# One kernel of a two-layer sequence model: compression, compressed attention and the choice of blocks written as one stage

## The chip, the cores and the metric

The kernel runs on one core of a Trainium2 chip. The metric is the device time of one launch in microseconds (us); lower is better.

## The reference

The whole model has two layers of attention and two feed-forward blocks on 1,024 tokens of width 1,024. The change touches one part of the second attention layer, whose 16 heads in 4 groups attend in three ways. The part in question is the compressed way and the choice of blocks:

```python
n_cmp = (S - CMP_LEN) // CMP_STRIDE + 1          # 63 windows of 32 tokens, one every 16
cidx = arange(n_cmp)[:, None] * CMP_STRIDE + arange(CMP_LEN)[None, :]
def compress(t, pe, w1, w2):                     # t: 4 groups x 1024 tokens x 64
    blocks = t[:, :, cidx] + pe
    blocks = blocks.reshape(Bn, C_KV_HEADS, n_cmp, CMP_LEN * HEAD_DIM)
    return silu(blocks @ w1) @ w2                # 2048 -> 128 -> 64
k_cmp = rms_norm(compress(kc, cmp_pe[0], cmp_w1[0], cmp_w2[0]), k_gain[0])
v_cmp = compress(vc, cmp_pe[1], cmp_w1[1], cmp_w2[1])
s_c = q @ k_cmp * scale - slopes * dist_c        # masked where dist_c < 0
p_c = softmax(s_c)                               # zero where a token sees no window
o_cmp = p_c @ v_cmp
importance = einsum('bgjtn,nm->bgtm', p_c, overlap)    # 16 blocks of 64 tokens
score = where(blk > cur, -inf, where(forced, inf, importance))
top_s, top_i = top_k(score, 8)                   # blocks for the selected attention
```

## The kernel before

The program is a row of stages. Each has its own buffers and semaphores, one instruction stream for each engine, and ends with a barrier of all engines, so that no stage overlaps the next. TensorE is "PE", VectorE "DVE", ScalarE "ACT", GpSimd "POOL", and SyncE "SP" issues most DMAs.

Between the projection stage `in1` and the attention stage `at1` of the second layer stand, in this order:

- three short mask stages (`distance_bias_stage`, and `bias_parts_stage` twice), which the change leaves as they are and only moves;
- `compress_stage` ("cmp"). SP loads `w1s` and `t_in` for keys and values. Both have the 64 channels of a head on 64 partitions. PE waits for all six loads, then multiplies each of the 32 steps of the window by the position embedding (`ps_b`, L1819, one moving column) and by the strided windows of the four groups (`ps_h`, L1825, 252 moving columns), for keys and for values. Each full fp32 matmul shows as two instructions in the trace. A short chain of Silu, the second matrix, the norm and a transposition gives `kcT` and `vc`;
- `select_stage` ("sel"). It handles one group (4 heads) and one tile of 128 tokens at a time: 32 rounds, with the tiles `n` and the groups in one order on every engine. `q` is loaded with 66 rows for each head (64 channels and two rows that carry the distance term). In each round PE makes `transposes(n)`, `values(n-1)`, `scores(n+2)`; DVE makes `normalize(n)`, from the fifth token tile on `pick(n)` (the sum over heads, the sum over windows, the eighth largest, the mark), `output(n-1)` and `negate(n+2)`; ACT makes four exponentials with their sums and one copy out of PSUM;
- `transposed_selection_stage` ("selT"), which transposes the marks of all tokens and stores them in DRAM for `at1` through the POOL queue.

The lines of the round are: L1954 scores, L1964 transposes, L1974 values, L2032 mask added, L2035 maximum, L2001 exponentials, L2046 probabilities, L2056 to L2072 the choice, L2081 the gated output.

Of the kernel before, what the change touches and what calls it, by code (L numbers as in the profile page):

```python
# [1751 lines left out]
def compress_stage(nc, kvT, pe, w1, w2, k_gain, gate_cols, kcT, vc, gates, ident):  # L1752


    G = KV_HEADS
    NW = N_CMP
    with Stage(nc, "cmp") as st:
        t_in = st.sb("t_in", [HD, 2, G, SEQ])
        w1s = st.sb("w1s", [HD, 2, CMP_LEN, CMP_HIDDEN])
# [10 lines left out]
        root = st.sb("root", [NW, G])  # L1770
        rstd = st.sb("rstd", [NW, G])
        pos_i = st.sb("pos_i", [CMP_PAD, 1], I32)
        ktok = st.sb("ktok", [CMP_PAD, G, HA])
        ps_h = st.ps("ps_h", [CMP_HIDDEN, 2, BANK])
        ps_b = st.ps("ps_b", [CMP_HIDDEN, 2, BANK])
        ps_c = st.ps("ps_c", [CMP_PAD, 2, BANK])
        ps_t = st.ps("ps_t", [P, 1, BANK])
        pe_in, in_sem, g_in, gain_in = st.sem("pe_in"), st.sem("in"), st.sem("g_in"), st.sem("gain_in")
        peT_ready, peT_done, bias_ready, pb_done, hid_ready, hid_done, c_ready = (
            st.sem(x) for x in ("peT_ready", "peT_done", "bias_ready", "pb_done", "hid_ready", "hid_done", "c_ready"))  # L1780
# [557 lines left out]
```

## Time and profile before

| | |
|---|---|
| median of three runs | 4008.2 us (4007.9 to 4011.0) |
| the profiled execution | 4013.1 us, of it 4011.1 us span |
| busy share of the span | PE 86%, weight loads (PEld) 72%, DVE 41%, ACT 30%, POOL 3% |
| `cmp`, first DMA to the next stage | 2173.1 to 2285.4 us |
| `sel` | 2285.4 to 2507.3 us |
| `selT`, up to the first instruction of `at1` | 2507.3 to 2519.2 us |
| mask stages ahead of `cmp` | 2161.7 to 2173.0 us |

Times are counted from the start of the span. The profile names each instruction by its line and its tiles, written out<-in. "PEclk" is the granted TensorE clock: 1.00 is 2.4 GHz and 0.50 is 1.2 GHz. Busy shares are averages over stages with different limits. Because a barrier closes each stage, the time of a stage is the time of its own longest chain.

### The profile page before, as it was taken

To read this page: it belongs to the slowest core of one execution; us is meant where nothing else is said; L and a number is where in the kernel's file an instruction comes from. 1 tells how busy PE (TensorE), PEld (TensorE's weight loads), DVE (VectorE), ACT (ScalarE), POOL (GpSimd) and SP (SyncE) were. 2 spreads that over 40 slices of the span, in tenths; PEclk is the share of its full clock that TensorE was granted. 3 is DMA by queue.
4 is the path that set the end of the run, shared out by engine and by line. 5 is a ranking of instruction groups with operands and counts; after the bars stand their busy time and mean duration, and the time that the engine had idled before them with its cause. 6 is when DMAs were issued, how large, how long until landed. Compare 5 with 4: busy or idle time off the path is not lost. (4 is left out here: it accounts for less than half of the span.)

```text
span 4011.1 us, 46382 instructions
## 1 busy us (share of the span) xinstructions
PE 3463.5 (86%) x17061; PEld 2898.9 (72%) x17061; DVE 1654.7 (41%) x3187; ACT 1222.4 (30%) x2492; POOL 118.3 (3%) x152
## 2 busy tenths in 40 slices
PE   5997673776889999997996877699999879999998
PEld 4886563665778888886886666588788668888887
DVE  3133784445223232324430044588788332323323
ACT  3233332333122121223331132466566222221211
POOL 0000000000000000000000000111111000000000
PEclk8998786888999999998995555899999989999999
DMA  3344001332022121212733000321120111212112
GB/s 116 100 106 113 16 6 40 68 64 67 6 63 74 58 70 57 74 45 62 175 91 66 22 22 0 65 62 32 33 63 1 42 48 53 74 53 79 63 59 84
DMA packets 262495, 239.79 MB, mean 60 GB/s; under 512 B 41928, under 2 KB 203720, under 8 KB 262280
## 3 DMA queue, kind: packets, MB, share of 16 engines
q1 hardware_dynamic: 262200, 236.67, 22.1%
q8 instruction: 135, 2.21, 0.2%
q0 software_dynamic: 80, 0.26, 0.1%
q14 instruction: 80, 0.66, 0.1%
HBM read 191.58 MB, written 45.29 MB: 59 GB/s over the span
## 5 line engine op out<-in xcount | busy, mean ns | idle before, releaser
L498 PE MATMUL ffn_acc<-ffn_hT_hi,ffn_w_hi 128*128 128x512 f32 x1408 | 435.9, 391 | 17.5 <-DVE ffn_w_lo L579 17.5
L498 PE MATMUL ffn_acc<-ffn_hT_lo,ffn_w_hi 128*128 128x512 f32 x1408 | 435.3, 390 | 0.0
L498 PE MATMUL ffn_acc<-ffn_hT_hi,ffn_w_lo 128*128 128x512 f32 x1408 | 434.8, 390 | 0.0
L579 DVE TENSOR_TENSOR ffn_w_lo<-ffn_raw,ffn_w_hi 128x1024 fp32r<-128x1024 f32 x88 | 107.9, 1226 | 738.5 <-ACT ffn_w_hi L538 738.5
L1153 PE MATMUL in_acc<-in_w_hi,hT_hi 128*128 128x512 f32 (+1 forms) x832 | 330.4, 397 | 14.8 <-DVE in_w_lo L1233 14.8
L1637 ACT ACTIVATE at_pr<-at_ps_s 128x512 f32<-128x512 f32 x480 | 224.2, 467 | 335.2 <-PE at_ps_s L1570 332.8
L1155 PE MATMUL in_acc<-in_w_hi,hT_lo 128*128 128x512 f32 (+1 forms) x832 | 325.6, 391 | 0.0
L1154 PE MATMUL in_acc<-in_w_lo,hT_hi 128*128 128x512 f32 (+1 forms) x832 | 324.9, 391 | 0.0
L538 ACT ACTIVATE ffn_w_hi<-ffn_raw 128x1024 fp32r<-128x1024 f32 x88 | 93.3, 1060 | 750.1 <-PE ffn_acc L498 737.2
L1696 DVE TENSOR_TENSOR at_p_lo<-at_pr,at_p_hi 128x512 fp32r<-128x512 f32 x480 | 273.0, 586 | 110.2 <-ACT at_p_hi L1644 109.7
L498 PEld LDWEIGHTS ffn_acc<-ffn_hT_hi,ffn_w_hi 128*128 128x128 f32 x1408 | 265.4, 189 | 73.1 <-DVE ffn_w_lo L579 18.1
L498 PEld LDWEIGHTS ffn_acc<-ffn_hT_lo,ffn_w_hi 128*128 128x128 f32 x1408 | 265.6, 189 | 55.5
L498 PEld LDWEIGHTS ffn_acc<-ffn_hT_hi,ffn_w_lo 128*128 128x128 f32 x1408 | 265.4, 189 | 55.3
L1686 DVE TENSOR_REDUCE at_top<-at_ps_m 128x1 f32<-128x512 f32 (+1 forms) x480 | 243.7, 526 | 129.6 <-PE at_ps_m L1550 126.5
L518 PE MATMUL ffn_acc_d<-ffn_d_hi,ffn_a_hi 128*128 128x512 f32 x704 | 273.9, 389 | 0.0
L519 PE MATMUL ffn_acc_d<-ffn_d_lo,ffn_a_hi 128*128 128x512 f32 x704 | 273.9, 389 | 0.0
L520 PE MATMUL ffn_acc_d<-ffn_d_hi,ffn_a_lo 128*128 128x512 f32 x704 | 273.9, 389 | 0.0
L1550 PE MATMUL at_ps_m<-at_kc,at_qa 128*128 128x512 f32 (+1 forms) x480 | 177.0, 382 | 112.0 <-DMA at_qb<-q0T_lo 37.3
L1644 ACT ACTIVATE at_p_hi<-at_pr 128x512 fp32r<-128x512 f32 x480 | 237.9, 497 | 0.0
L1550 PEld LDWEIGHTS at_ps_m<-at_kc,at_qa 128*128 128x128 f32 x480 | 95.1, 198 | 143.8 <-issue 83.4
L1153 PEld LDWEIGHTS in_acc<-in_w_hi,hT_hi 128*128 128x128 f32 x832 | 165.5, 199 | 45.6 <-DVE in_w_lo L1233 17.1
L549 ACT ACTIVATE ffn_d_hi<-ffn_d_raw 128x512 fp32r<-128x512 f32 x176 | 108.4, 629 | 277.9 <-PE ffn_acc_d L520 277.9
(307 smaller groups left out, 6090.8 us busy)
## 6 DMA issues: line engine op xcount, KB each, us to landing
ffn_d_raw<-in_ffn_w_down SPq DMA_DIRECT2D x176, 256.0 KB, 2.8
ffn_raw<-in_ffn_w_gate SPq DMA_DIRECT2D x44, 512.0 KB
ffn_raw<-in_ffn_w_up SPq DMA_DIRECT2D x44, 512.0 KB
in_raw<-in_hy_w_in SPq DMA_DIRECT2D x56, 256.0 KB
proj<-in_nat SPq DMA_DIRECT2D x40, 256.0 KB, 2.1
in_raw<-in_nsa_w_in SPq DMA_DIRECT2D x40, 256.0 KB
sel_q<-q1T SPq DMA_DIRECT2D x16, 264.0 KB
at_qa<-q1T_hi SPq DMA_DIRECT2D x16, 264.0 KB
```

The costliest lines, as they stand in the source:

```text
L498: ins = nc.tensor.matmul(acc[:, m, half, :], w[:, m, k, :], h[:, k, half * HALF:(half + 1) * HALF], start=k == 0 and w is w_hi and h is hT ...
L518: nc.tensor.matmul(acc_d[:, x, :], a_hi[:, k, rows], d_hi[:, n % R, :], start=k == 0, stop=False)
L519: nc.tensor.matmul(acc_d[:, x, :], a_hi[:, k, rows], d_lo[:, n % R, :], start=False, stop=False)
L520: ins = nc.tensor.matmul(acc_d[:, x, :], a_lo[:, k, rows], d_hi[:, n % R, :], start=False, stop=k == G - 1)
L1153: nc.tensor.matmul(acc[:, n % 4, 0:cols], x_hi, r_hi, start=k == 0, stop=False)
L1154: nc.tensor.matmul(acc[:, n % 4, 0:cols], x_hi, r_lo, start=False, stop=False)
L1155: ins = nc.tensor.matmul(acc[:, n % 4, 0:cols], x_lo, r_hi, start=False, stop=k == KD - 1)
L1550: ins = nc.tensor.matmul(ps_m[:, m % 2, pos * P:(pos + n) * P], lhsT, rhs, start=x == 0, stop=x == len(parts) - 1, skip_group_check=True)
L1637: nc.scalar.activation(pr[:, c % R, 0:w], ps_s[:, c % RB, 0:w], ACT.Exp).then_inc(p_done, 1)
L1644: nc.scalar.activation(p_hi[:, c % R, 0:w], pr[:, c % R, 0:w], ACT.Copy).then_inc(hi_done, 1)
L1686: ins = nc.vector.tensor_reduce(top[:, u, half, x:x + 1], ps_m[:, m % 2, 0:w * P], AX.X, ALU.max)
L1696: nc.vector.tensor_tensor(p_lo[:, c % R, 0:w], pr[:, c % R, 0:w], p_hi[:, c % R, 0:w].bitcast(F32), ALU.subtract).then_inc(lo_done, 1)
```

## The change

The three stages become one, `compress_select_stage` ("cmpsel"), which stands ahead of the mask stages.

- Compression works with 128 rows: steps 0 to 15 of the window on partitions 0 to 63 and steps 16 to 31 on partitions 64 to 127. For that `t_in` holds the tokens twice, the second time shifted by 16. There are 16 matmuls for keys and 16 for values, each with 258 moving columns: 256 windows and two columns for the position embedding. Keys have their own wait (`k_in`), and values theirs (`v_in`).
- `q` holds two heads on 128 partitions, without the rows of the distance term. `kcp` and `vcp` hold the compressed keys and values of a group twice, block-diagonally, so that one matmul of 128x128 serves two heads.
- A round is a tile of 128 tokens with all 16 heads: 8 rounds instead of 32. Each has 8 head pairs in `scores`, `transposes` and `values`, and DVE works on 128x1024 elements at a time.
- The distance term is made by POOL (`make_bias`) and added by DVE. POOL subtracts the maximum, ACT makes one exponential of 128x1024, and DVE sums it with a reduction.
- `ps_t` and `ps_o` are no longer doubled; `ps_s` is.
- The marks are transposed for the last four token tiles only, and stored through the SP queue inside the same stage.

```diff
...
+def compress_select_stage(nc, kvT, pe, w1, w2, k_gain, gate_cols, qT, gates, selT, mixed, ident, slopes):
...
+        t_in = st.sb("t_in", [P, 2, COLS + 2 * HALF])
+        w1s = st.sb("w1s", [P, 2, HALF, CMP_HIDDEN])
...
+        kcp = st.sb("kcp", [P, G, P])
+        vcp = st.sb("vcp", [P, G, P])
+        q = st.sb("q", [P, PAIRS, SEQ])
...
+        ps_s = st.ps("ps_s", [P, 2, 2 * BANK])
+        ps_t = st.ps("ps_t", [P, 2, BANK])
+        ps_o = st.ps("ps_o", [P, 2, BANK])
...
+            for v, done in ((0, k_in), (1, v_in)):
+                kv = kvT[v * G:(v + 1) * G, 0:HD, :].rearrange("g r t -> r g t")
+                to = t_in[:, v, 0:COLS].rearrange("p (g t) -> p g t", g=G)
+                wv = w1[v, :, :].rearrange("(e l d) h -> e d l h", e=2, d=HD)
+                for half in range(2):
+                    rows = slice(half * HD, half * HD + HD)
+                    sp.dma_start(w1s[rows, v, :, :], wv[half]).then_inc(done, 16)
+                    sp.dma_start(to[rows, :, 0:SEQ - half * HALF], kv[:, :, half * HALF:SEQ]).then_inc(done, 16)
...
+            for n in range(2):
+                tok = slice(n * BANK, (n + 1) * BANK)
+                for half in range(2):
+                    of = qT[:, 0:HD, tok].rearrange("(j e) r t -> e r j t", e=2)[half]
+                    sp.dma_start(q[half * HD:half * HD + HD, :, tok], of).then_inc(q_in[n], 16)
+            sp.wait_ge(selT_taken, 1)
+            sp.wait_ge(blocks_set, 1)
+            sp.dma_start(selT.rearrange("g b t -> (g b) t"), blocks[:].bitcast(F32)).then_inc(sel_out, 16)
+            sp.wait_ge(sel_out, 16)
...
+            def make_bias(i):
...
+                nc.gpsimd.tensor_tensor(bias[:, i % 2, :, :],
+                                        dist[:, i % 2, :].rearrange("p (o n) -> p o n", o=1).to_broadcast([P, C_HEADS, CMP_PAD]),
+                                        bcast(nslope[:].rearrange("p (h o) -> p h o", o=1), CMP_PAD), ALU.mult).then_inc(bias_step, 1)
+                pool.wait_ge(bias_step, i + 1)
+                nc.gpsimd.affine_select(out=bias[:, i % 2, :, :], in_=bias[:, i % 2, :, :], compare_op=ALU.is_ge, fill=NEG,
+                                        base=i * P - (CMP_LEN - 1), pattern=[[0, C_HEADS], [-CMP_STRIDE, CMP_PAD]],
+                                        channel_multiplier=1).then_inc(bias_done, 1)
...
+            make_bias(0)
+            make_bias(1)
+            for i in range(TT):
+                pool.wait_ge(top1_done, i + 1)
+                nc.gpsimd.tensor_tensor(s[:, i % 2, :, :], s[:, i % 2, :, :],
+                                        bcast(top1[:, i % 2, :].rearrange("p (h o) -> p h o", o=1), CMP_PAD), ALU.subtract)\
+                    .then_inc(sub_done, 1)
+                if i + 2 < TT:
+                    make_bias(i + 2)
...
+            for v, done in ((0, k_in), (1, v_in)):
+                te.wait_ge(done, 64)
+                for l in range(HALF):
+                    windows = t_in[:, v, l:l + CMP_STRIDE * (NW + 1) + 1:CMP_STRIDE]
+                    ins = nc.tensor.matmul(ps_s[:, 0, v * BANK:v * BANK + NW + 2], w1s[:, v, l, :], windows, start=l == 0,
+                                           stop=l == HALF - 1)
...
+            def scores(i):
+                if i % 4 == 0:
+                    te.wait_ge(q_in[i // 4], 32)
+                if i >= 2:
+                    te.wait_ge(biased, i - 1)
+                for m in range(PAIRS):
+                    ins = nc.tensor.matmul(ps_s[:, i % 2, m * P:(m + 1) * P], q[:, m, i * P:(i + 1) * P], kcp[:, m // 2, :],
+                                           start=True, stop=True)
+                ins.then_inc(s_done, 1)
+
+            def transposes(i):
+                te.wait_ge(pn_done, i + 1)
+                if i:
...
+                for m in range(PAIRS):
+                    ins = nc.tensor.transpose(ps_t[:, m // 4, (m % 4) * P:(m % 4 + 1) * P], rows[:, m, :], ident[:])
+                ins.then_inc(t_done, 1)
...
+            def values(i):
+                te.wait_ge(pt_done, i + 1)
...
+                for m in range(PAIRS):
+                    ins = nc.tensor.matmul(ps_o[:, m // 4, (m % 4) * P:(m % 4 + 1) * P], pt[:, i % 2, m, :], vcp[:, m // 2, :],
+                                           start=True, stop=True)
+                ins.then_inc(o_done, 1)
+
+            scores(0)
+            scores(1)
+            for i in range(TT):
+                transposes(i)
+                if i:
+                    values(i - 1)
+                if i + 2 < TT:
+                    scores(i + 2)
+            values(TT - 1)
+            te.wait_ge(biased, TT)
+            te.wait_ge(sel_done, TT - FIRST)
+            for i in range(FIRST, TT):
+                ins = nc.tensor.transpose(ps_s[0:G * N_SLC, 0, (i - FIRST) * P:(i - FIRST + 1) * P],
+                                          sel[:, i - FIRST, :, :].rearrange("p g n -> p (g n)"), ident[:])
+            ins.then_inc(selT_ready, 1)
...
+                    nc.scalar.activation(hid_v[:, :, 0, :], of.rearrange("p (g n) -> p g n", g=G), ACT.Silu, bias=pb[:, 1:2])
+                    nc.scalar.activation(hid_v[:, :, 1, :], of.rearrange("p (g n) -> p g n", g=G), ACT.Silu, bias=pb[:, 1:2])\
...
+            nc.scalar.activation(gates[:], g_raw[:], ACT.Sigmoid).then_inc(norm, 1)
+            act.wait_ge(c_ready, 2)
+            act.wait_ge(zeroed, 2)
+            for half in range(2):
+                rows = slice(half * HD, half * HD + HD)
+                nc.scalar.activation(vcp[rows, :, rows], ps_o[rows, 1, 0:G * HD].rearrange("p (g d) -> p g d", d=HD), ACT.Copy)\
+                    .then_inc(vcp_done, 1)
+
+            def exps(i):
+                act.wait_ge(sub_done, i + 1)
+                nc.scalar.activation(s[:, i % 2, :, :], s[:, i % 2, :, :], ACT.Exp).then_inc(e_done, 1)
...
+                nc.scalar.activation(pt[:, i % 2, :, :], ps_t[:].rearrange("p b (m c) -> p (b m) c", c=P), ACT.Copy).then_inc(pt_done, 1)
...
+            act.wait_ge(selT_ready, 1)
+            act.wait_ge(blocks_set, 1)
+            nc.scalar.activation(blocks[:, FIRST * P:SEQ], ps_s[0:G * N_SLC, 0, 0:SEQ - FIRST * P], ACT.Copy).then_inc(selT_taken, 1)
...
+            dve.wait_ge(norm, 4)
+            nc.vector.reciprocal(rstd[:], root[:]).then_inc(norm, 1)
+            dve.wait_ge(norm, 5)
+            for half in range(2):
+                ins = nc.vector.tensor_tensor(ktok[:, :, half, :], ps_o[0:CMP_PAD, 0, 0:G * HD].rearrange("p (g d) -> p g d", d=HD),
+                                              bcast(rstd[:].rearrange("p (g o) -> p g o", o=1), HD), ALU.mult)
...
+            for half in range(2):
+                rows = slice(half * HD, half * HD + HD)
+                nc.vector.tensor_scalar(kcp[rows, :, rows], ps_t[rows, 0, 0:NW].rearrange("p (g n) -> p g n", n=CMP_PAD),
+                                        gain[rows, 0:1], None, ALU.mult).then_inc(kcp_done, 1)
...
+            def maxima(i):
+                dve.wait_ge(s_done, i + 1)
+                dve.wait_ge(bias_done, i + 1)
...
+                nc.vector.tensor_tensor(s[:, i % 2, :, :], ps_s[:, i % 2, :].rearrange("p (h n) -> p h n", n=CMP_PAD),
+                                        bias[:, i % 2, :, :], ALU.add).then_inc(biased, 1)
...
+                nc.vector.tensor_reduce(top1[:, i % 2, :], s[:, i % 2, :, :], AX.X, ALU.max).then_inc(top1_done, 1)
...
+            def normalize(i):
...
+                nc.vector.tensor_reduce(rowsum[:, i % 2, :], s[:, i % 2, :, :], AX.X, ALU.add).then_inc(link, 1)
+                dve.wait_ge(link, at + 1)
+                nc.vector.reciprocal(rl[:, i % 2, :], rowsum[:, i % 2, :]).then_inc(link, 1)
...
+                nc.vector.tensor_tensor(pn[:, i % 2, :, :], s[:, i % 2, :, :],
+                                        bcast(rla[:, i % 2, :].rearrange("p (h o) -> p h o", o=1), CMP_PAD), ALU.mult)\
+                    .then_inc(pn_done, 1)
...
+            def pick(i):
...
+                nc.vector.tensor_reduce(both[:, :, 1:], pn[:, i % 2, :, :].rearrange("p (g j) n -> p g n j", g=G), AX.X, ALU.add)\
...
+            def output(i):
+                dve.wait_ge(o_done, i + 1)
...
+                nc.vector.tensor_tensor(mixed[:, i, :].rearrange("p (h d) -> p h d", d=HD),
...
+            maxima(0)
+            maxima(1)
+            for i in range(TT):
+                normalize(i)
+                if i >= FIRST:
+                    pick(i)
+                if i:
+                    output(i - 1)
+                if i + 2 < TT:
+                    maxima(i + 2)
+            output(TT - 1)
...
+                compress_select_stage(nc, kvT, nsa_cmp_pe[0, :, :, :], nsa_cmp_w1[0, :, :, :], nsa_cmp_w2[0, :, :, :],
+                                      nsa_k_gain[0, 0, :], proj1[:, main:ODD_IN], q1T, gates, selT, mixed, ident,
+                                      slopes(C_HEADS, 0, C_HEADS))
                 masks = []
...
-                compress_stage(nc, kvT, nsa_cmp_pe[0, :, :, :], nsa_cmp_w1[0, :, :, :], nsa_cmp_w2[0, :, :, :],
-                               nsa_k_gain[0, 0, :], proj1[:, main:ODD_IN], kcT, vc, gates, ident)
-                select_stage(nc, q1T, kcT, vc, gates, sel, mixed, ident)
...
-                transposed_selection_stage(nc, sel, selT, ident)
...
```

The seven operations of `pick(i)` are those of before on 128x4x64 and 128x4x16 elements; `max` and `match_replace` run four times, once for each group.

## Rows read from the trace of the kernel before

**Rows 1.** The page's slices: the granted clock in 40 equal slices.

```profile
PEclk8998786888999999998995555899999989999999
```

**Rows 2.** Windows by stage: length, busy us (instructions), clock, DMA share, GB/s.

```profile
core 0: us, PE busy (x) PEld busy (x) DVE busy (x) ACT busy (x) POOL busy (x), PEclk, DMA share, GB/s
2173.00:2197.80 24.80, 0.31 (x1) 0.13 (x1) 0.22 (x1) 0.00 (x0) 1.36 (x12) 0.50 1.00 181
2197.80:2225.10 27.30, 27.27 (x128) 27.27 (x129) 0.00 (x0) 0.00 (x0) 0.00 (x0) 0.50 0.00 1
2225.10:2279.90 54.80, 54.80 (x130) 39.07 (x131) 0.00 (x0) 1.95 (x4) 0.00 (x0) 0.50 0.00 0
2279.90:2285.40 5.50, 2.47 (x20) 2.04 (x20) 1.97 (x6) 4.12 (x6) 0.00 (x0) 0.50 0.00 0
2293.40:2507.30 213.90, 153.14 (x640) 130.74 (x640) 92.70 (x320) 66.09 (x289) 0.00 (x0) 0.50 0.05 14
```

**Rows 3.** Timeline of one of 32 rounds: start, us, engine, line, operation, idle before.

```profile
2489.53 0.43 DVE L2046 TENSOR_TENSOR sel_pn<-sel_e,sel_rla 128x256 f32<-128x256 f32 x1
2489.99 0.60 DVE L2056 TENSOR_REDUCE sel_both<-sel_pn 128x64 f32<-128x256 f32 x1
2490.11 1.03 PE L1964 MATMUL sel_ps_t<-ident,sel_pn 128*64 128x128 f32 x4 [1.88 <-DVE sel_pn L2046]
2491.07 1.97 PE L1974 MATMUL sel_ps_o<-vc,sel_pt 64*128 x8
2492.05 0.17 DVE L2072 TENSOR_SCALAR sel<-sel_marked 128x16 f32 x1 [0.15 <-DVE sel_marked L2070]
2492.97 1.97 PE L1954 MATMUL sel_ps_s<-kcT,sel_q 66*128 x8
2494.97 0.42 DVE L2032 TENSOR_TENSOR sel_s<-sel_ps_s,sel_cmask 128x256 f32<-128x256 f32 x1 [1.33 <-PE sel_ps_s L1954]
2496.24 0.43 DVE L2046 TENSOR_TENSOR sel_pn<-sel_e,sel_rla 128x256 f32<-128x256 f32 x1
```

**Rows 4.** Windows: the transfer rate of the first loads, nothing else running.

```profile
2176.00:2196.00 20.00, 0.00 (x0) 0.00 (x0) 0.21 (x1) 0.00 (x0) 0.00 (x0) 0.50 1.12 205
```

**Rows 5.** Timeline: the end of `cmp`, table load and sigmoid.

```profile
2282.84 1.28 ACT L1853 ACT_TABLE_LOAD   x1
2284.13 0.52 ACT L1853 ACTIVATE gates<-cmp_g_raw 128x384 f32<-128x384 f32 x1
```

**Rows 6.** Groups by form, whole kernel: busy us, mean ns, idle before.

```profile
L920 DVE TENSOR_TENSOR hg_q<-hg_ps_tr,hg_q 128x1024 f32<-128x1024 f32 x4 | 4.9, 1225 | 5.5 <-ACT hg_q L845 5.5
L1240 DVE TENSOR_REDUCE in_ss<-in_sq 128x8 f32<-128x512 f32 x32 | 22.0, 687 | 86.2 <-ACT in_sq L1195 86.2
L1529 POOL TENSOR_TENSOR at_shift<-ident,at_top 128x512 fp32r<-128x512 f32 x80 | 91.5, 1143 | 747.1 <-DVE at_top L1690 747.1
L1520 POOL TENSOR_SCALAR_AFFINE_SELECT at_base<-at_base 128x1024 f32<-128x1024 f32 x2 | 2.1, 1038 | 0.1
L838 ACT ACTIVATE hg_kl<-hg_kl 128x1024 f32<-128x1024 f32 x4 | 4.2, 1056 | 0.1
```

**Rows 7.** Windows in other stages, for the clock.

```profile
424.40:428.20 3.80, 3.80 (x18) 3.80 (x19) 0.00 (x0) 0.00 (x0) 0.00 (x0) 0.50 0.02 4
428.20:442.00 13.80, 13.71 (x124) 13.52 (x123) 6.60 (x12) 5.15 (x7) 0.00 (x0) 1.00 0.01 2
473.20:482.30 9.10, 0.00 (x0) 0.00 (x0) 8.98 (x15) 0.03 (x1) 0.00 (x0) 0.66 0.64 173
1857.00:1865.20 8.20, 6.80 (x30) 6.00 (x31) 7.39 (x11) 3.58 (x6) 0.00 (x0) 0.50 0.01 2
1865.20:1868.90 3.70, 1.71 (x13) 1.24 (x12) 3.70 (x5) 2.27 (x4) 0.00 (x0) 0.96 0.00 0
```

**Rows 8.** Timeline: the marks' store and the next stage.

```profile
2513.92 0.69 POOL L2188 DMA_DIRECT2D selT<-selT_blocks  x1 [226.39 <-ACTq L67]
2519.15 0.94 POOL L1515 MEMSET at_base<- 128x1024 f32 x1 [4.54 <-POOLq L70]
```

More of the change, by code:

```diff
@@ L1747, in _ @@
             rounds(dve, body)
[L1752 to L1759, printed above, removed]
+def compress_select_stage(nc, kvT, pe, w1, w2, k_gain, gate_cols, qT, gates, selT, mixed, ident, slopes):
+    G, J = KV_HEADS, GROUP
+    HALF = CMP_LEN // 2
+    COLS = G * SEQ
+    NW = G * CMP_PAD
+    PAIRS = C_HEADS // 2
+    FIRST = TOPN * SLC // P
+    PICKED = 3e38
+    FORCED = 1e30
+    with Stage(nc, "cmpsel") as st:
+        t_in = st.sb("t_in", [P, 2, COLS + 2 * HALF])
+        w1s = st.sb("w1s", [P, 2, HALF, CMP_HIDDEN])
@@ L1770, in compress_stage @@
[L1770 to L1780, printed above, removed]
@@ L1812, in _ @@
             te.wait_ge(pe_in, 16)
-            nc.tensor.transpose(ps_t[0:HD, 0, 0:2 * CMP_LEN], pes[:], ident[0:2 * CMP_LEN, 0:2 * CMP_LEN]).then_inc(peT_ready, 1)
-            te.wait_ge(in_sem, 16 * 6)
-            te.wait_ge(peT_done, 1)
-            for v in range(2):
-                for l in range(CMP_LEN):
-                    ins = nc.tensor.matmul(ps_b[:, v, 0:1], w1s[:, v, l, :], peT[:, v * CMP_LEN + l:v * CMP_LEN + l + 1],
-                                           start=l == 0, stop=l == CMP_LEN - 1)
-                ins.then_inc(bias_ready, 1)
@@ L1822, in _ @@
[L1822 to L1833 removed]
+            for v in range(2):
+                ins = nc.tensor.transpose(ps_t[:, 1, v * HALF:(v + 1) * HALF], pes[:, v, :, :].rearrange("l e d -> l (e d)"),
+                                          ident[0:HALF, 0:HALF])
@@ new lines, in _ @@
+            te.wait_ge(w2_in, 16)
+            te.wait_ge(hid_done, 1)
+            for g in range(G):
+                ins = nc.tensor.matmul(ps_o[0:CMP_PAD, 0, g * HD:(g + 1) * HD], hid_k[:, g, :], w2s[:, 0, :], start=True, stop=True)
+            ins.then_inc(c_ready, 1)
+            te.wait_ge(hid_done, 2)
+            for g in range(G):
+                ins = nc.tensor.matmul(ps_o[:, 1, g * HD:(g + 1) * HD], hid_v[:, g, :, :].rearrange("p e n -> p (e n)"), w2s[:, 1, :],
+                                       start=True, stop=True)
```

421 lines of the change are left out of this document (147 added, 274 removed).

## The prediction
> **What bounds the kernel now.** I read the page's slices first, then windows cut at the stage borders, then the timeline of one round. The slices put four tenths of a millisecond at half clock [rows 1]: it is this part of the program. The windows then say what each stage waits for [rows 2]. First 24.8 us of transfers with PE idle; then 27.3 and 54.8 us in which PE is busy throughout at clock 0.50; a chain of 5.5 us; and 213.9 us of rounds in which PE is busy for 153.1 us and no other engine for more than 92.7. With the load of `q` and `selT` it is 346.1 us, from 2173.0 to 2519.15 [rows 8]. A barrier closes every stage, so what is saved here is saved in the total.
>
> The round shows why PE at 72% still sets the pace [rows 3]. `pn` ends at 2489.96; PE transposes, multiplies values and makes scores until 2494.94; then DVE adds the mask, takes the maximum and normalizes, and `pn` ends again at 2496.67. The period is 6.7 us: about 5.0 on PE, then 1.7 on DVE, with neither covering the other. 32 x 6.7 = 214. The choice (`pick`), 2489.99 to 2492.22, lies under PE's part and costs nothing.
>
> **The front.** The new stage begins with its loads. Before, 4.28 MB landed in 24.8 us; at 205 GB/s [rows 4] that is 20.9 us, and 3.8 to start and finish. Keys now need 2 x 0.52 MB of `w1s` and 2 x 1.05 MB of `t_in`, the second copy at full price: 3.16 MB, 15.4 + 3.8 = 19.2 us. Values end at 6.3 MB: 30.7 + 3.8 = 34.5 us. The load grows by 10 us, but the keys' matmuls now lie under it. `q` (two parts of 2.1 MB) lands at 46 and 56 us, before it is wanted.
>
> PE loses the 128 instructions of `ps_b` (27.3 us) for two more moving columns in each other matmul. Of the 128 instructions of `ps_h`, 0.428 us each [rows 2], 64 remain with 258 columns, 0.438 each at half clock: 14.0 us for keys and 14.0 for values. Keys are done at 33.2 us even so, under the load of values; the values' batch is on the path.
>
> What is its clock? The old batches, with 64 rows, stayed at 0.50 for 82 us of unbroken work [rows 2]. An earlier stage with full fp32 matmuls of 128x128 began at 0.50 and was at 1.00 after 3.8 us [rows 7]; after PE's last work at 473.2 it fell again (a mean of 0.66 over 9.1 us is 2.9 us at 1.00). The new batch has 128 rows, so it is nearest to the latter. I take 5 us at half clock (11 instructions) and 21 at 0.219: 9.5 us, between 7.0 and 14.0.
>
> The chain behind it took 5.5 us, its barrier included. It gains a second Silu, a second `ktok` and `kcp` (0.42 to 0.5 each), and a wait: the reciprocal now waits for `norm` at 4, which the sigmoid of the gates completes, so its table load and itself (1.28 + 0.52) [rows 5] enter the chain. Behind the waiting DVE stand `ktok`, the transposes and every score. With the barrier gone I take 8.0. Scores start at 34.5 + 9.5 + 8.0 = 52 us.
>
> **A round.** At 128x1024 a DVE operation costs 1.23 us, from PSUM too; a reduction, 0.69 at 512, as much [rows 6]. `maxima` is two of them, 2.5 us; `normalize` two with two small ones, 3.0 us; `output` 1.25. `pick` takes 2.2 now for one group; its long reduction, 0.60 at 256 elements, becomes 1.95 at 1024 (1.2 if it runs as a plain one, 2.4 if it scales), the rest doubles with four `max` and `match_replace`: 5.1 us. POOL's two-input operation takes 1.14 us for 512 columns, so 2.3 for each of the two long ones, 1.04 for the select and 0.4 for two small ones: 6.1 us a round, under the 12 us of the others. ACT has 1.06 for the exponential and as much for the copy out of `ps_t`; that tile is single now, but the copy is done long before the next transposes, under values and scores.
>
> PE issues 8 transposes, 16 instructions of values and 16 of scores. They go at 0.214 us each at half clock (1.97 for 8) [rows 3], and half of that at full. The order on each engine is as before, so the lockstep is too: after `pn` PE has all 40, and only then can DVE take the new maxima and normalize. At half clock 9.2 + 5.5 = 14.7 us, at full 4.6 + 5.5 = 10.1, or 11.85 where `pick` and `output` (6.35) outlast PE. But PE rests for the 5.5 us, and 2.9 us of rest were enough to lose the clock [rows 7]; so each burst starts at half. With 5 us of that (23 instructions) and 17 at 0.107, plus 0.4, it is 7.2 us and the period 12.7. `pick` stays hidden: values are done at 5.4.
>
> The Trainium skill, in "TensorE: Matmul & The Clock Gate", Part 4, says that transposes do not count as activity for the clock. Here PE did only transposes from 1857.0, and the clock rose at 1865.2 [rows 7], so the trace disagrees. By the page each burst would begin with 1.7 us that do not count; about 0.9 us more a round, 3834 us in all.
>
> **The sum.** First tile: scores 3.6, maxima 2.5, POOL's subtraction 2.3, a table load 1.3 and the exponential 1.1, normalize 3.0: 13.8. Round 0 has no values: 5.2 + 5.5 = 10.7. Rounds 1 to 5: 5 x 12.7 = 63.5. Round 6 has no maxima: `pick`, `output`, normalize, 9.4. That is 97.4. The tail: `output(6)` ends at 6.7 (5.4 + 1.25); the last values wait for it, since `ps_o` is single; 2.8; the four transposes 0.8; the copy 0.7; and from the store to the next stage 5.2 [rows 8]: 16.2. The stage: 52 + 97.4 + 16.2 = 165.6 us for 346.1, a saving of 180.5.
>
> The moved mask stages cost what they cost, 11.4 us; they touch no queue of this stage. `at1` starts cold either way, after the same kind of barrier, and reads `selT` as before. The store leaves POOL's queue for SP's, at the same price. The sum is made against the profiled execution, 4013.1 us (span 4011.1), and gives 3832.6; that execution lies 4.9 over the median, so the forecast is 4008.2 - 180.5 = 3828.
>
> **The rivals.**
>
> (B) The clock never rises in the rounds, as in the old ones at 72% busy [rows 2]. For it: PE is busy for 9.2 of 14.7 us, less than before. Against it: 128 rows instead of 64. Values 14.0; the rounds 13.8 + 11.2 + 5 x 14.7 + 9.9 = 108.4; the tail 17.6: with 34.5 + 14.0 + 8.3, 182.8 us. Saving 163.3: 3845.
>
> (C) The clock stays high between bursts. Batch 7.0 and chain 7.9; rounds 12.1 + 8.3 + 3 x 10.1 + 2 x 11.85 + 9.4 = 83.8; tail 14.8: 148 us, saving 198: 3810. Against it: the rest of 5.5 us.
>
> (D) The load or an engine is slower than its row on top of B. In the loads of `at1` the rate fell to 165 GB/s; 6.3 MB at that rate is 7.5 us more; `pick` at its upper bound and POOL at twice its price on the first tile add 2 to 3: 3855.
>
> (E) Slower than before: POOL paces the rounds. The subtraction of each tile and two steps of the next bias stand in one queue, and DVE, ACT and PE all wait for them. The Trainium skill, "GPSIMD Engine Reference", Engine selection, advises against two-input elementwise work there. Up to 5.6 us for each of the two long ones it stays hidden (2 x 5.6 + 1.4 = 12.6); for no gain a round would need 12.7 + 180/7 = 38 us, or 18 us each. The row has 2.3.
>
> That the change does not do what it says is hardly open: fewer rounds and rows are in the instructions. DMA time hidden anyway is no case either, since nothing overlaps the stage.
>
> **How the numbers follow.** Forecast 0.50 (its own range 3818 to 3838), B 0.25, C 0.10, D 0.14, E 0.01. The range takes in B and most of D above, and C below: 3808 to 3854. A difference of 0.2% (8 us) is about what a measurement of this kernel can tell from none. Every case but E is faster by far more: faster 0.98, same 0.01, slower 0.01.
>
> **What would show it.** The keys' matmuls start 19 us and the values' 34 to 35 us after the first DMA. `kcp` follows 8 us after the last of them and waits for the sigmoid. Eight rounds have a period of 12 to 13 us, each with a PE burst that starts at 0.50 and ends at 1.00 and a rest of 5.5 us. DVE never waits for POOL after the first tile. From the first DMA to the mask stages it is about 166 us. I am wrong if `pick` ends behind the values, if the load takes more than 36 us, if the subtraction costs over 5 us, or if the clock does not move.

## The result, and the profile after

| | before | after |
|---|---|---|
| median | 4009.6 us (4 runs, 4007.9 to 4015.3) | 3831.8 us (4 runs, 3828.9 to 3835.5) |
| the profiled execution | 4013.1 us, span 4011.1 | 3828.9 us, span 3827.1 |

The ratio is 0.9555, its 95% interval 0.9538 to 0.9571. The forecast was 3828, in a range of 3808 to 3854: the change saves 177.8 us by the medians, and 180.5 were forecast.

The slices of the kernel after, to be laid beside [rows 1]: the four slices at half clock are gone.

```profile
PEclk9999787799889999999899676999999989999999
```

The windows of the new stage, cut at its own borders: length, busy us (instructions), clock, DMA share, GB/s. They answer to [rows 2].

```profile
core 0: us, PE busy (x) PEld busy (x) DVE busy (x) ACT busy (x) POOL busy (x), PEclk, DMA share, GB/s
2154.30:2172.80 18.50, 0.39 (x2) 0.28 (x2) 0.82 (x24) 0.20 (x1) 10.04 (x32) 0.50 0.96 187
2172.80:2187.10 14.30, 14.22 (x32) 7.92 (x32) 0.00 (x0) 0.01 (x1) 0.00 (x0) 0.80 1.09 200
2188.40:2202.60 14.20, 14.12 (x33) 7.27 (x33) 0.00 (x0) 0.64 (x2) 0.00 (x0) 0.88 1.07 207
2202.60:2210.20 7.60, 2.43 (x21) 1.97 (x20) 2.46 (x7) 6.49 (x11) 0.00 (x0) 0.71 0.86 168
2210.20:2309.00 98.80, 50.70 (x280) 49.08 (x280) 67.05 (x105) 15.63 (x15) 40.23 (x32) 0.72 0.00 0
2309.00:2323.00 14.00, 7.84 (x44) 7.31 (x44) 6.56 (x19) 1.61 (x2) 0.03 (x1) 0.74 0.09 19
```

Read down: the keys' loads; the keys' batch; the values' batch; the chain up to the first score; first tile and rounds; the tail. It is 168.7 us where 346.1 stood before. The second and third lines hold the one surprise: the 32 instructions of a batch take 14.2 us in both, though the clock is at 0.80 and 0.88 on the mean.

The front, from timelines of the kernel after (PE first, then the chain):

```profile
2172.83 14.22 PE L1898 MATMUL cmpsel_ps_s<-cmpsel_t_in,cmpsel_w1s 128*128 128x258 f32 x32 [16.38 <-DMA cmpsel_t_in<-kvT]
2188.48 14.15 PE L1898 MATMUL cmpsel_ps_s<-cmpsel_t_in,cmpsel_w1s 128*128 128x258 f32 x32 [1.43 <-DMA cmpsel_t_in<-kvT]
...
2205.51 1.28 ACT L1985 ACT_TABLE_LOAD   x1
2206.80 0.52 ACT L1985 ACTIVATE gates<-cmpsel_g_raw 128x384 f32<-128x384 f32 x1
...
2207.36 0.17 DVE L2030 RECIPROCAL cmpsel_rstd<-cmpsel_root 64x4 f32<-64x4 f32 x1 [2.74 <-ACT gates L1985]
```

Values start 1.43 us behind the end of the keys, when their load lands. The reciprocal sits idle for 2.74 us and is released by the sigmoid of the gates, which has nothing to do with it: the wait that came with the changed semaphore count.

One round, tile 2, from a timeline of the kernel after; it answers to [rows 3].

```profile
2248.44 1.97 PE L1934 MATMUL cmpsel_ps_t<-ident,cmpsel_pn 128*128 128x128 f32 x8 [5.85 <-DVE cmpsel_pn L2069]
2250.20 3.58 PE L1944 MATMUL cmpsel_ps_o<-cmpsel_vcp,cmpsel_pt 128*128 128x128 f32 x16
2253.61 1.95 PE L1924 MATMUL cmpsel_ps_s<-cmpsel_kcp,cmpsel_q 128*128 128x128 f32 x16
...
2255.60 1.23 DVE L2049 TENSOR_TENSOR cmpsel_s<-cmpsel_ps_s,cmpsel_bias 128x1024 f32<-128x1024 f32 x1 [0.56 <-PE cmpsel_ps_s L1924]
2256.86 1.22 DVE L2052 TENSOR_REDUCE cmpsel_top<-cmpsel_s 128x16 f32<-128x1024 f32 x1
2258.00 1.21 DVE L2057 TENSOR_REDUCE cmpsel_rowsum<-cmpsel_s 128x16 f32<-128x1024 f32 x1
2259.24 0.25 DVE L2059 RECIPROCAL cmpsel_rl<-cmpsel_rowsum 128x16 f32<-128x16 f32 x1
2259.53 0.57 DVE L2065 COPY cmpsel_rla<-cmpsel_rl 128x16 f32<-128x16 f32 x1
2260.13 1.23 DVE L2069 TENSOR_TENSOR cmpsel_pn<-cmpsel_s,cmpsel_rla 128x1024 f32<-128x1024 f32 x1
```

And the clock of that round, in windows (columns as above):

```profile
2248.30:2250.40 2.10, 1.96 (x9) 1.97 (x10) 0.08 (x1) 0.00 (x0) 2.02 (x2) 0.50 0.00 0
2250.40:2253.60 3.20, 3.20 (x17) 3.20 (x16) 0.00 (x0) 1.02 (x1) 1.21 (x2) 0.50 0.00 0
2253.60:2255.60 2.00, 1.96 (x18) 1.77 (x16) 1.22 (x2) 0.00 (x0) 0.00 (x0) 1.00 0.00 0
2255.60:2261.40 5.80, 0.00 (x0) 0.00 (x0) 5.62 (x6) 1.06 (x1) 3.17 (x3) 0.92 0.00 0
```

It is the lockstep of before on a larger tile: PE 7.2 us, then DVE 5.8 us with PE idle. Sixteen instructions of 128x128 (the values) take 3.58 us at half clock up to their last, and sixteen more (the scores) 1.95 at full clock.

The choice, which stands in rounds 4 to 6 and in the tail, lies under PE in rounds 5 and 6. In round 4 it does not quite, from PE's and DVE's timelines of the kernel after:

```profile
2276.46 2.44 PE L1944 MATMUL cmpsel_ps_o<-cmpsel_vcp,cmpsel_pt 128*128 128x128 f32 x16
2279.58 0.20 DVE L2097 TENSOR_SCALAR cmpsel_sel<-cmpsel_marked 128x64 f32<-128x64 f32 x1
2286.93 1.97 PE L1934 MATMUL cmpsel_ps_t<-ident,cmpsel_pn 128*128 128x128 f32 x8 [6.24 <-DVE cmpsel_pn L2069]
```

There the clock rose early and the values were done at 2278.90, 0.9 us before the choice ended at 2279.78. PE then rested for 6.24 us instead of 5.84.

POOL and DVE in the first tile, from two timelines of the kernel after:

```profile
2222.21 1.90 POOL L1879 TENSOR_TENSOR cmpsel_s<-cmpsel_s,cmpsel_top 128x1024 f32<-128x1024 f32 x1
...
2221.19 1.08 DVE L2063 TENSOR_SCALAR cmpsel_rla<-cmpsel_rl,cmpsel_alive 128x16 f32<-128x16 f32 x1
2222.31 2.88 DVE L2069 TENSOR_TENSOR cmpsel_pn<-cmpsel_s,cmpsel_rla 128x1024 f32<-128x1024 f32 x1
```

The product `pn` takes 2.88 us instead of 1.23: it starts 0.1 us behind a POOL operation of 1.90 and ends 1.1 after it, nearly its own length. No idle time shows; the wait is inside the instruction.

The end of the stage, which answers to [rows 8]: the store now leaves from SP, and the next stage begins 4.05 us later instead of 5.2.

```profile
2318.92 0.51 SPq L1837 DMA_DIRECT2D selT<-cmpsel_blocks  x1
2322.97 0.95 POOL L2179 MEMSET causal<- 128x1024 f32 x1 [24.88 <-DVEq L67]
```

### The profile page after: what moved, and what is told of

It reads as the page before. It is cut to its first block and busy times, and to the rows that moved or that the text cites. A ratio compares the mean times of both kernels' runs of the same rounds, so it can differ in the third digit from the quotient of the medians.

```text
span 3827.1 us, 44401 instructions
## 1 busy us (share of the span) xinstructions
PE 3307.1 (86%) x16522; PEld 2768.0 (72%) x16522; DVE 1634.9 (43%) x2991; ACT 1171.4 (31%) x2221; POOL 164.8 (4%) x197
## 5 line engine op out<-in xcount | busy, mean ns | idle before, releaser
L498 PEld LDWEIGHTS ffn_acc<-ffn_hT_hi,ffn_w_hi 128*128 128x128 f32 x1408 | 265.1, 188 | 73.5 <-DVE ffn_w_lo L579 18.5
L498 PEld LDWEIGHTS ffn_acc<-ffn_hT_hi,ffn_w_lo 128*128 128x128 f32 x1408 | 264.9, 188 | 55.2
L1550 PE MATMUL at_ps_m<-at_kc,at_qa 128*128 128x512 f32 (+1 forms) x480 | 177.2, 382 | 104.2 <-DMA at_qb<-q0T_lo 34.3
```

The source lines that it names most:

```text
L498: ins = nc.tensor.matmul(acc[:, m, half, :], w[:, m, k, :], h[:, k, half * HALF:(half + 1) * HALF], start=k == 0 and w is w_hi and h is hT ...
L1550: ins = nc.tensor.matmul(ps_m[:, m % 2, pos * P:(pos + n) * P], lhsT, rhs, start=x == 0, stop=x == len(parts) - 1, skip_group_check=True)
```

## The experiments

All but e9 are edits of the kernel after. A difference of a few us between two launches is noise of the whole kernel, so small effects are read in the trace, in the stage alone. Even there the values' load ends at 33.0 to 34.2 us, and the front varies with it by up to 1.2 us. "Front" is from the stage's first instruction to the first score, "rounds" from there to the last `pn`, "tail" from there to the next stage.

| | front | rounds | tail | stage | launch |
|---|---|---|---|---|---|
| after | 55.9 | 98.7 | 14.0 | 168.7 | 3831.8 |
| e1_contig | 50.2 | 98.0 | 14.0 | 162.2 | 3822.1 (one run) |
| e2_stride4 | 55.7 | 99.0 | 14.0 | 168.7 | 3834.5 (one run) |
| e4_nocopy | 55.7 | 96.4 | 13.8 | 165.9 | 3825.2 (one run) |
| e6_gates_store | 53.3 | 98.0 | 14.6 | 165.9 | 3828.5 (one run) |
| e5_filler | 55.1 | 92.5 | 13.1 | 160.7 | 3822.8 (one run) |
| e7_ahead | 55.2 | 68.4 | 20.8 | 144.4 | 3806.7 |
| e8_ahead_all | 52.9 | 66.8 | 20.8 | 140.5 | 3801.5 |
| e10_act_sums | 53.5 | 60.2 | 19.5 | 133.2 | 3798.7 |
| e11_repacked | 49.0 | 60.2 | 20.8 | 129.9 | 3791.4 |

### Which part saves what: e9_cmp_only

The kernel before, with `compress_stage` alone rewritten for 128 rows (`t_in`, `w1s` and the two batches as in the change's diff) and its Silu reading 63 of every 64 columns.

> The kernel before with only the compression changed: 128-row packing, 16 matmuls each for keys and values with own waits, tokens loaded twice; select stage and order of stages as before. Theory (the saving is the sum of a front and of rounds): from the first DMA to the next stage 34.2 + 14.2 + 5.9 = 54.3 us instead of 112.3, saving 58 us, 3951 us (ratio 0.9855); the other 119 us of the 177 belong to the rounds and the tail. Rival (the front's gain depends on the fusion, since a barrier and the load of q stand behind it either way): saving under 45 us.

3947.8 us, ratio 0.985 (0.9834 to 0.9866). The first load and the first load of the next stage, in the timeline of SyncE's queue:

```profile
2168.85 0.34 SPq L1788 DMA_DIRECT2D cmp_pes<-in_nsa_cmp_pe  x1
...
2223.05 3.10 SPq L1932 DMA_DIRECT2D sel_q<-q1T  x8
```

54.2 us for 112.3. The packing saves 58 us without any of the rest (61 by the medians of whole launches). By subtraction the other 119 us belong to what this run leaves out. Of them 8.0 are the time from the end of `cmp` to the first score, in which `q` was loaded (2285.4 to 2293.4 in [rows 2]); the front, with 55.9 us for 54.2, gives 1.7 back; the rest, 113 us, lies in the wider rounds and the tail. No run takes these apart further.

### What holds the compression batches: e1_contig and e2_stride4

```diff
-                    windows = t_in[:, v, l:l + CMP_STRIDE * (NW + 1) + 1:CMP_STRIDE]
+                    windows = t_in[:, v, l:l + NW + 2]                       # e1_contig
+                    windows = t_in[:, v, l:l + 4 * (NW + 1) + 1:4]           # e2_stride4
```

> The windows of the compression matmuls are read as 258 neighbouring elements instead of every 16th; the output is then not the reference's. Theory S (the step of 16 elements holds the moving rows at one rate, whatever the clock): once the clock is at 1.00 the instructions of L1898 stand 0.22 us apart instead of 0.434; with some 11 of 32 at half clock a batch takes 9.4 us instead of 14.2, and scores start 4.7 us earlier after the first DMA (51 us instead of 55.9). Rival W (the instruction itself, weights and 258 columns, takes 0.434 us whatever it reads): the batches stay at 14.2 us and the stage keeps its 168.6 us.

> The windows are read with a step of 4 elements (16 bytes) instead of 16 (64 bytes); the output is not the reference's. If any step but one costs the half rate: batches of 14.2 us as in the kernel after. If only a large step costs it: 9.4 us as with neighbouring elements. In between: 0.3 us an instruction, 10 to 12 us a batch.

The values' batch in PE's timeline of e1_contig, and then of e2_stride4:

```profile
2191.25 9.56 PE L1898 MATMUL cmpsel_ps_s<-cmpsel_t_in,cmpsel_w1s 128*128 128x258 f32 x32 [4.83 <-DMA cmpsel_t_in<-kvT]
```

```profile
2196.72 14.83 PE L1898 MATMUL cmpsel_ps_s<-cmpsel_t_in,cmpsel_w1s 128*128 128x258 f32 x32 [0.24 <-DMA cmpsel_t_in<-kvT]
```

With neighbouring elements the values' batch takes 9.6 us, as my sum had it (9.5). With a step of 64 bytes it takes 14.2, and with 16 bytes 14.8, though the clock is at 1.00 for much of the batch in all three, in e2_stride4 for all of it. So it is the step: at full clock the instructions stand 0.22 us apart with neighbouring elements (2196.3 to 2200 in e1_contig), 0.44 with the step of 64 bytes, and 0.46 with 16 bytes. At half clock the step of 64 bytes costs nothing that shows: 0.43 us apart with it (the keys' first instructions in the kernel after) and 0.43 without (the same in e1_contig). That is why [rows 2], all at half clock, could not tell. The batch explains 4.6 of the 5.7 us by which the front of e1_contig is shorter; the other 1.1 are a load that ended earlier. (The rounds of e1 were 0.7 us shorter as well; they vary by that much between kernels that leave them alone.)

The Trainium skill, "SBUF — State Buffer", Door 1, says that memory lines are 16 bytes, that at least two accesses must hit one for full rate, and that one may therefore step 4 fp32 elements for free. The first half fits the runs, though none has a step of 2, where exactly two elements share a line. The conclusion does not: a step of 4 elements was as slow as one of 16.

### Where POOL disturbs DVE: e4_nocopy

```diff
-                    nc.vector.tensor_copy(rla[:, i % 2, :], rl[:, i % 2, :]).then_inc(link, 1)
...
-                                        bcast(rla[:, i % 2, :].rearrange("p (h o) -> p h o", o=1), CMP_PAD), ALU.mult)\
+                                        bcast(per_head[:, i % 2, :].rearrange("p (h o) -> p h o", o=1), CMP_PAD), ALU.mult)\
```

`per_head` is `rl` from the second tile on.

> From the second tile on the probabilities are scaled straight by rl, and the copy of 16 elements into rla (0.57 us in a round, 0.17 where POOL is idle) is gone. Theory L (the copy is long only because it waits for POOL's operation of 1.90 us to end): what follows it waits in its place; the reciprocal or the product with rl takes the 0.4 us, so a round gets 0.15 to 0.2 us shorter and 7 rounds 1.2 us. Rival C (the copy itself is slow): 0.57 + 0.04 us a round, 4.2 us over 7 rounds, stage 164.4 instead of 168.6.

From timelines of e4_nocopy, DVE and POOL:

```profile
2249.62 1.62 DVE L2068 TENSOR_TENSOR cmpsel_pn<-cmpsel_s,cmpsel_rl 128x1024 f32<-128x1024 f32 x1
...
2248.26 1.90 POOL L1879 TENSOR_TENSOR cmpsel_s<-cmpsel_s,cmpsel_top 128x1024 f32<-128x1024 f32 x1 [5.83 <-DVE cmpsel_top L2052]
```

The copy of 16 elements is gone, and `pn` grew from 1.23 to 1.62: it starts before POOL's operation ends at 2250.16, and comes out 0.39 longer. Most of the copy's length was a wait, and it moved. The rounds got 2.3 us shorter where theory L had 1.2 and its rival 4.2. Round 3 alone was 1.7 us shorter (11.6 for 13.3) and rounds 4 and 5 together 0.9 longer, so the total decides nothing between the two; the length of `pn` does. The Trainium skill, "SBUF — State Buffer", "SBUF: two separate sides", describes it: a DVE operation with two SBUF inputs shares a pair of ports with a GpSimd operation that reads SBUF, and so does a DVE operation in a two-port mode, such as an fp32 copy within SBUF; the pair is a lock, held for the whole instruction. The first tile (2.88 us) agrees with it. The sums and maxima of a tile, with one input, stayed at 1.21 to 1.22 us beside POOL.

### The wait for the gates, and the store's queue: e6_gates_store

```diff
-            nc.scalar.activation(gates[:], g_raw[:], ACT.Sigmoid).then_inc(norm, 1)
+            nc.scalar.activation(gates[:], g_raw[:], ACT.Sigmoid).then_inc(gates_set, 1)
...
-            dve.wait_ge(norm, 4)
+            dve.wait_ge(norm, 3)
...
-            sp.dma_start(selT.rearrange("g b t -> (g b) t"), blocks[:].bitcast(F32)).then_inc(sel_out, 16)
+            pool.dma_start(selT.rearrange("g b t -> (g b) t"), blocks[:].bitcast(F32)).then_inc(sel_out, 16)
```

> Two edits that are read apart. (1) The sigmoid of the gates signals its own semaphore, and the reciprocal of the norm waits only for the root. Theory: rstd started 2.74 us late, of it 1.8 for table load and sigmoid (1.28 + 0.52); the chain from the last values' matmul to the first score goes from 7.6 to 5.8 us. Rival: the table load and the sigmoid only move behind, and vcp or kcp waits for them: 7.6 as before. (2) The marks are stored through POOL's queue instead of SP's. Theory (the queue sets the price): 5.2 us from the store to the next stage, as in the kernel before, instead of 4.05. Rival (the other layout of the store made it shorter): 4.05.

```profile
2208.34 0.17 DVE L2031 RECIPROCAL cmpsel_rstd<-cmpsel_root 64x4 f32<-64x4 f32 x1 [0.91 <-ACT cmpsel_root L1984]
...
2319.49 0.72 POOL L1883 DMA_DIRECT2D selT<-cmpsel_blocks  x1 [20.83 <-ACT cmpsel_blocks L2011]
2323.80 0.95 POOL L2180 MEMSET causal<- 128x1024 f32 x1 [3.60 <-DVEq L67]
```

These rows are of e6's timeline. (1) The reciprocal is 0.91 us late instead of 2.74, and the chain from the last values' matmul to the first score takes 5.8 us instead of 7.6, as the theory had it. (The front is 2.6 us shorter; the other 0.8 are an earlier load.) (2) The store from POOL's queue costs 4.3 us from its issue, and 4.6 from the end of the copy ahead of it, against 4.05 and 4.07 from SP's. So the queue accounts for 0.3 to 0.5 us, and neither theory holds whole. The rest of the 1.2 us by which it was faster than in [rows 8], also from POOL's queue, is not settled: the store has 64 rows where there were 16, and another stage follows it.

### Does the clock set the length of the burst: e5_filler

```diff
+                if i + 1 < TT:
+                    te.wait_ge(pt_done, i + 1)
+                    for _ in range(4):
+                        nc.tensor.matmul(ps_t[:, 0, :], ident[:], q[:, 0, 0:BANK], start=True, stop=True)
```

> In the rest of each round PE multiplies the identity by 512 columns of q four times into the already taken transposes' PSUM (fp32, eight instructions), which nothing reads. Theory (each burst begins at half clock because PE rested for 5.8 us): the clock stays at 1.00 in the burst, the burst shrinks from 7.2 to 4.7 us where pn waits for it; rounds without pick 10.5 to 11 instead of 12.5 us; rounds with pick go to 12.2 at most, since pick, values' take and output (6.35) now outlast PE's burst; together some 9 us less in the rounds, stage 160. Rival (the bursts' length is set by the weight loads and by PE's own rate, not by the clock): no round is shorter, and filler that stands in the way of the transposes costs 0 to 1 us each, stage 168 to 176.

PE's timeline of a round of e5_filler, and the windows of this round and the next:

```profile
2249.70 1.09 PE L1934 MATMUL cmpsel_ps_t<-ident,cmpsel_pn 128*128 128x128 f32 x8 [2.41 <-DVE cmpsel_pn L2073]
2250.63 1.95 PE L1944 MATMUL cmpsel_ps_o<-cmpsel_vcp,cmpsel_pt 128*128 128x128 f32 x16
2252.41 1.95 PE L1924 MATMUL cmpsel_ps_s<-cmpsel_kcp,cmpsel_q 128*128 128x128 f32 x16
2254.20 3.60 PE L1959 MATMUL cmpsel_ps_t<-cmpsel_q,ident 128*128 128x512 f32 x8
```

```profile
2249.70:2260.20 10.50, 8.10 (x48) 5.83 (x48) 6.84 (x7) 2.08 (x2) 6.26 (x6) 1.00 0.00 0
2260.20:2272.30 12.10, 9.73 (x48) 7.47 (x48) 6.84 (x7) 2.08 (x2) 6.23 (x6) 0.86 0.00 0
```

In this round, with most of PE's rest filled, the clock is 1.00 throughout, values take 1.95 us instead of 3.58, the burst is 4.7 us and the round 10.5 instead of 13.0. Rounds 4 and 5, with the choice, take 12.2 us. So the clock does set the burst's length, and work that computes nothing gives 6.3 us in the rounds and 8.0 in the stage (0.9 of them in the front, which the edit leaves alone). It does not hold the clock every time. The last window is round 3, without a choice too, in which the clock fell to 0.86 on the mean although PE had rested for 2.41 us as ahead of round 2; in round 5 it fell to 0.86 as well, after 4.13 us of rest. Why it fell in one round and not in the other after the same rest is open.

### Taking the lockstep away: e7_ahead and e8_ahead_all

```diff
             for i in range(TT):
+                if i + 2 < TT:
+                    scores(i + 2)
                 transposes(i)
                 if i:
                     values(i - 1)
-                if i + 2 < TT:
-                    scores(i + 2)
...
+            normalize(0)
             for i in range(TT):
-                normalize(i)
+                if i + 2 < TT:
+                    maxima(i + 2)
+                if i + 1 < TT:
+                    normalize(i + 1)
                 if i >= FIRST:
                     pick(i)
                 if i:
                     output(i - 1)
-                if i + 2 < TT:
-                    maxima(i + 2)
```

> The order is shifted by one tile: PE makes scores(i+2), transposes(i), values(i-1); DVE makes maxima(i+2), normalize(i+1), pick(i), output(i-1). Same instructions. Theory (a round is PE's burst plus DVE's rest because each waits for the other in turn): with the tiles apart the round is the longer of the two. DVE has 2.45 + 3.3 + 1.25 = 7.0 us without pick and 11.5 to 12 with it; PE 4.6 to 9.2. Tiles 0 to 3: 7.5 to 9.5 instead of 12.3; tiles 4 to 7: 12 instead of 12.5. Some 15 to 20 us less, 3814 us, ratio to before 0.951. Rival (DVE and POOL are the bound, PE is hidden anyway): at most 2 us less, 3830. Rival (the new order makes PE wait for the bias or the pick): rounds of 15 us, 3845.

3806.7 us, ratio 0.9494 (0.9478 to 0.951). A window of e7_ahead over rounds 0 to 4 (columns as above):

```profile
2232.00:2266.00 34.00, 24.76 (x184) 23.09 (x184) 33.05 (x34) 11.05 (x11) 30.70 (x24) 0.91 0.00 1
```

DVE has almost no idle time left (busy for 33.05 of 34.00 us), and a round takes 6.5 to 6.8 us where it took 10.9 to 13.3. The clock is at 0.91 over these rounds without any filler. The rounds give 30.3 us; 6.8 come back in the tail, where PE's last values now wait behind two choices. With 0.7 from the front that is 24.3 us in the stage (25.1 by the medians), above what I expected: I had put all tiles with a choice at 12 us, and only two choices lie in the rounds (11.3 and 8.8 us), the other two in the tail.

> The shifted order of e7_ahead with the two small edits beside it: the gates' own semaphore and no rla copy. If the parts add up: front 2.6 us shorter (53.3 for 55.9), and in the rounds, which DVE now bounds, the copy's 0.57 or 1.22 us is gone, while the product with rl may take 0.4 more where POOL is busy: 0.2 to 0.8 us a round, 1.4 to 5.6 in seven. Stage 136 to 140 us for 144.4, median 3801. Rival (the copy only absorbed the wait for POOL, all of it comes back in the product): stage 141.8, 3804.

3801.5 us (0.9461 to 0.949), stage 140.5. The front is 2.3 us shorter. Without the copy a round takes 6.3 to 6.6 us instead of 6.5 to 6.8, because `pn` takes 1.62 or 2.27 instead of 1.23: the parts add up as the wait for POOL lets them. The stage lies between what I had expected (136 to 140) and the rival (141.8).

### Work moved from DVE and POOL to ACT: e10_act_sums

On top of e8_ahead_all; POOL's subtraction and DVE's row sum are gone, and DVE's maximum is negated.

```diff
-                nc.scalar.activation(s[:, i % 2, :, :], s[:, i % 2, :, :], ACT.Exp).then_inc(e_done, 1)
+                for h in range(C_HEADS):
+                    ins = nc.scalar.activation(s[:, i % 2, h, :], s[:, i % 2, h, :], ACT.Exp, bias=top1[:, i % 2, h:h + 1],
+                                               accum_out=rowsum[:, i % 2, h:h + 1])
```

> The shifted order, the gates' own semaphore, no rla copy, and the softmax moved: DVE makes the negated maximum, ACT makes 16 exponentials of 128x64 with the maximum as bias and the row sum as second output, POOL subtracts nothing and DVE has no sum. DVE a round: 2.45 + 1.7 + 1.25 = 5.4 us, with pick 9.8; ACT 16 x 0.33 (from the rows of before) + 1.0 = 6.3 to 9.3 if the read of each sum (0.19) adds to it. Theory (DVE is the bound once the lockstep is broken, and POOL's subtraction costs it waits as well): rounds of 6.5 to 9.3 without pick, 10 with it; stage some 130 to 140 us for 168.6, 3800 us. Rival (ACT takes over as the bound at 9.3 us or more, and the sixteen small operations cost what the large one saved): no better than the shifted order alone, 3814.

3798.7 us (0.9456 to 0.9487), stage 133.2. A window of e10_act_sums:

```profile
2230.00:2255.00 25.00, 19.45 (x144) 18.32 (x144) 19.76 (x20) 24.98 (x135) 15.57 (x16) 0.90 0.00 1
```

ACT is busy for 24.98 of 25.00 us: it is the bound here, at some 6.3 us a round (16 exponentials 0.33 us apart, the read of each sum lying under the next, and the copy of 1.0). The rounds with a choice are still DVE's (9.5 and 7.1 us). Theory and rival were each half right: 11 us better in the stage than the order alone (8 by the medians), and the bound went to ACT. Against e8_ahead_all, on which it is built, the stage gains 7.3 us, and the medians, whose intervals overlap, only 2.8; the gain of this edit is read from the stage.

### A version that repairs the front too: e11_repacked

On top of e10_act_sums. `rows_of` shares its memory with `pn` and `pt`.

```diff
+                    te.wait_ge(packed, v * HALF + l + 1)
+                    windows = rows_of[:, l, :]
...
+                for l in range(HALF):
+                    nc.vector.tensor_copy(rows_of[:, l, :], t_in[:, v, l:l + CMP_STRIDE * (NW + 1) + 1:CMP_STRIDE]).then_inc(packed, 1)
```

> As e10_act_sums, and DVE copies the windows of each step (258 elements, every 16th) to neighbouring places ahead of the matmul that reads them; the copies share memory with pn and pt. The output is the reference's. Theory (the step of the moving operand sets the rate of L1898 at full clock, and DVE's copy of a step takes at most 0.45 us): the values' batch takes 9 to 10 us instead of 14.2, and the first copy adds 0.3; the front is 4 to 5 us shorter than in e10_act_sums (53.5), the median 3794. Rival (DVE reads every 16th element slowly too, above 0.9 us a copy): no gain, 3799 or more.

3791.4 us over 5 runs, ratio to before 0.9454 (0.9441 to 0.9466): the fastest of all. From timelines of e11_repacked, DVE and PE:

```profile
2189.65 4.88 DVE L2035 COPY cmpsel_flat<-cmpsel_t_in 128x258 f32<-128x258 f32 x16 [10.73 <-DMA cmpsel_t_in<-kvT]
...
2190.19 8.74 PE L1898 MATMUL cmpsel_ps_s<-cmpsel_flat,cmpsel_w1s 128*128 128x258 f32 x32 [5.91 <-DVE cmpsel_flat L2035]
```

DVE reads every 16th element at 0.31 us a copy of 258, so it runs ahead of PE, and the values' batch takes 8.7 us for 14.2. The front is 4.5 us shorter than in e10_act_sums: 5.4 from the batch, less a first copy of 0.5 ahead of it and a load that ended 0.6 later, and 0.2 from the chain behind.

## Why the prediction was right, and where its terms were off

The mechanism and the chosen case held: 3831.8 for 3828. By its own steps, predicted and measured in the profile after:

- **The load.** Keys 19.2, measured 18.5; values 34.5, measured 34.2. The rate of [rows 4] and the overhead of 3.8 us carried over.
- **The values' batch**, the term that was mis-sized: 9.5 us, measured 14.2. I took the clock as its only limit. The clock did rise, the rate did not, because of the 64-byte step (e1, e2). The stage was 3.1 us longer than forecast: 4.7 from this term, and 1.6 back from the others together. That they partly cancel is luck.
- **The chain** 8.0, measured 7.6; the wait for the sigmoid is there and costs 1.8 (e6).
- **The first tile** 13.8, measured 14.9. Behind it stands a cost that I did not have at all: DVE's `pn` and the small operation ahead of it lose 2.5 us to POOL (1.08 for some 0.2, 2.88 for 1.23). Against it stand the table load of 1.3, which lay under the transposes, and the subtraction with 1.90 for 2.3.
- **The rounds.** Round 0: 10.7, measured 10.9. Rounds 1 to 5: 63.5, measured 63.3, each between 12.2 and 13.3 us. Round 6: 9.4, measured 9.6. Burst 7.2 and rest 5.5, measured 7.2 and 5.8 in the round shown; over rounds 1 to 5 the burst was 6.0 to 7.4. Of the rest, 0.4 is the copy's wait for POOL. That the burst starts at half clock and ends at full was the claim on which the forecast stood against B and C, and both windows and e5 show it. That it would be at half clock for 5 us was an estimate. Single bursts differ by up to 1.4 us, so that the five rounds together came within 0.2 us is partly luck. The price of 0.214 us an instruction does not follow from the 1.97 us for 8 that I gave as its source (that is 0.246); it came out right all the same, 16 values at half clock standing 0.213 us apart. The choice took 4.3 to 5.0 us for 5.1 predicted, its reduction 1.92 to 1.95 for 1.95. It stayed hidden in rounds 5 and 6. In round 4 it ended 0.9 us behind the values, which I had named as a sign of being wrong, and cost 0.4 us: the clock rose early there, and a product of 64 elements took 0.93 us beside POOL's select for 0.28 without it.
- **The tail** 16.2, measured 14.0: the store 4.05 us for 5.2, and the last values 2.0 us at full clock for 2.8.
- **The stage** 165.6, measured 168.7 us. The mask stages took 11.7 us at their new place for 11.4. From the first instruction of what moved to `at1` it is 180.3 us for 357.5, a saving of 177.2, against 177.8 by the medians. The profiled executions differ by 184.3: another 7 us were there before the changed code was reached, and they are no part of it.

The rivals. B, a cold clock in the rounds, and D are out by the windows. C, a warm clock, did not happen, and e5 shows what came of a clock that is warm in most rounds: 6.3 us in the rounds, against the 13.6 by which C's sum lay lower. The first bursts are cold in it too, and two rounds lost their clock. E had the right resource with the wrong effect: POOL's subtraction takes 1.90 us, paces nothing, but it holds up DVE inside DVE's own instructions. "DVE never waits for POOL after the first tile" is true of the chain of waits and false of the durations: the copy into `rla` has 0.57 us in six rounds for 0.17 where POOL is idle. The reading that transposes do not count for the clock, which I weighed at 0.9 us more in a round, has no support here: rounds 1 to 5 came out 0.2 us under the sum without it.

## What to carry to other kernels

A wider tile divides the number of turns that two engines take in waiting for each other, but not the waiting itself: eight rounds in place of 32 still left PE idle for 5.8 of 13 us in each. Look in one round for the engine whose idle time ends exactly when the other's work ends, and shift the order by one tile; that was worth 24 us in this stage, more than filler work for the clock (8 us) or any single operation. And where a batch is to run at full clock, first ask whether its operands can be read at that rate: a limit that equals the slow clock's rate can't be seen before the clock rises.
